# The first FFN block's plain product, its two weights and the left sums moved ahead, around the last dense unit

## Chip, cores and metric

One core of a Trainium2 (trn2) chip. The metric is device time of one execution in microseconds (us), the median of several runs; lower is better. Times inside an execution are us from its first instruction.

## The reference, cut to what matters

Two layers, 256 tokens, model width 2048, FFN width 5632, all float32. Each layer is a mixer followed by a SwiGLU FFN, with RMS norms around both.

```python
def swiglu(h, w_gate, w_up, w_down):
    return (jax.nn.silu(h @ w_gate) * (h @ w_up)) @ w_down

for layer in range(DEPTH):
    h = rms_norm(x, norm_mix_pre[layer])
    m = ...                                  # even_mixer or diff_attention_mixer
    x = x + rms_norm(m, norm_mix_post[layer])
    h = rms_norm(x, norm_ffn_pre[layer])
    f = swiglu(h, ffn_w_gate[layer], ffn_w_up[layer], ffn_w_down[layer])
    x = x + rms_norm(f, norm_ffn_post[layer])
```

## The kernel before

**Units.** All weights go by in tiles of 512x512 floats (1 MB). Every tile that TensorE (PE) uses is a numbered unit `u`, and each unit passes the same chain: SyncE's queue (SP) loads it into a raw buffer (`load`, line 770); ScalarE (ACT) rounds it into `w_hi` (`hi`, line 901); VectorE (DVE) puts the remainder into `w_lo` (`lo`, line 1495); PE multiplies `w_hi` with the high part of the activations, `w_lo` with the high part, and `w_hi` with the low part, in this order. A dense unit (`product`, line 1225) does this for both halves of the tokens (24 matmuls), a single product (`single`, line 1246) for one (12 matmuls). PE, ACT, DVE, POOL (GpSimd) and SP each run their own list of instructions strictly in order, and wait for one another by counters. `hi(u)` waits for the unit four before to be done, `lo(u)` for the unit three before.

**The FFN of a layer.** The 5632 columns are 11 blocks of 512. The first block is the head: eight dense units, `head[0..3]` for gate and `head[4..7]` for up (512 rows each). The other ten are bodies (`Body`, line 105) of fifteen entries each, `ENTRIES` (line 98): row blocks 0 and 1 of gate and up, for the first and the second 128 tokens, make a 2x2 by 2x2 block product that is computed with seven single products instead of eight, P1 to P7; row blocks 2 and 3 go through the dense units g2, g3, u2, u3; then d0 to d3 add the previous block's down product.

- The plain products P1, P2, P3 use the weight tiles g0, g1, u1 as loaded. P5, P6, P7, P4 use differences that DVE forms in place (`form`, line 1502): P5 from u0 - g0 in g0's buffer, P6 and P4 from that buffer again, P7 in u0's buffer. So g0's buffer is in use from P1 until the remainder of P4 has been taken.
- P5, P6, P7, P3 need sums of activations, S1 to S4 (the left sums). For the first body POOL computes all of them in one task (`left_sums`, line 1971: eight operations of 128x512, in the order S1, S3, S2, S4), ACT takes the high parts (`left_high`, line 1115), DVE the low parts (`left_low`, line 1525). POOL starts as soon as the norm's scale is there, whatever the place in the task list; the place counts for ACT and DVE.

**The order around the change.** It is written out by a planner. `head_end` (line 294) lists the tasks of `head[4..7]`, which every engine then filters for its own. For DVE the list is: remainder of `head[6]`; of `head[7]`; then in the slot of `head[6]` remainder of P1, form P5, remainder of P5; in the slot of `head[7]` left lows S1 and S3, then `gate_up` (line 1767, the product of silu(gate) and up into `tok`), left lows S2 and S4. After it comes the first body's own list (`block`, lines 1780 to 1857): form P6, remainders of P3, P6, g2, form P7, an addition, remainder of P2, form P4, remainders of P7, P4, u3, and so on. PE's order is `head[7]`, P1, P5, eight transposes of `tok` (`turn`, line 1426), P3, P6, g2, P2, P7, P4, u3, g3, u2, d0 to d3.

**Loads.** SP issues the loads in one order: the head's as its slots come, then `gains` (a broadcast vector into `gq`), then `LOADS` (line 99) of each body: u1, u0, g0, g2, g1, u3, g3, u2, d0, d1, d3, d2. `place_loads` (line 505) gives each load the buffer whose last load was taken longest ago: three raw buffers for the dense units, five in the bodies (the three, and `gx` and `queries`, which the attention uses before). A load waits until the buffer's former tile is no longer needed; for g0 that is the remainder of P4, for u1 the remainder of P3 and form P7, for u0 the remainder of P7, for a plain tile its own remainder. In the first body u1 and u0 go to `gx` and `queries`, g0, g2, g1 to the raw buffers, and u3 follows u1 in `gx`, g3 follows u0, u2 follows g0.

Of the kernel before, what the change touches and what calls it, by code (L numbers as in the profile page):

```python
# [31 lines left out]
P = 128  # L32
# [3 lines left out]
KC = 512  # L36
# [60 lines left out]

ENTRIES = ("P1", "P5", "P3", "P6", "g2", "P2", "P7", "P4", "u3", "g3", "u2", "d0", "d1", "d2", "d3")
LOADS = ("u1", "u0", "g0", "g2", "g1", "u3", "g3", "u2", "d0", "d1", "d3", "d2")
FORMS = ("P5", "P6", "P7", "P4")  # L100
SUMS = ("S2", "S3")
PLAIN = {"P1": "g0", "P2": "g1", "P3": "u1"}
# [2 lines left out]
class Body:  # L105


    def __init__(self, layer, j, index, u, n, e, m, n_head):

        self.layer, self.j, self.index, self.first = layer, j, index, j == 0  # L110
        self.base, self.e, self.m = u, e, m
        self.u = {name: u + i for i, name in enumerate(ENTRIES)}
        self.up, self.gate, self.down = n, n + 1, n + 2
        self.head_up, self.next = n_head + 1, None
        self.form = {name: len(FORMS) * index + i + 1 for i, name in enumerate(FORMS)}
        self.sum = {name: len(SUMS) * index + i + 1 for i, name in enumerate(SUMS)}


class Part:
# [174 lines left out]
def head_end(slots, body):  # L294

    def left(name):
        return Task("sums", 2 * body.layer + 1, body.layer, what=name)

    tasks = []
    for i, s in enumerate(slots):  # L300
        last = len(slots) - 1 - i
        tasks += half(s, 0)
        tasks += [hi(u) for u in range(ahead(s.u - 1, HI_LEAD), min(ahead(s.u, HI_LEAD), body.base + 1))]
        tasks += [lo(u) for u in range(ahead(s.u - 1, LO_LEAD), min(ahead(s.u, LO_LEAD), body.base + 1))]
        if last == 1:
            tasks += [Task("form", src=body, what="P5"), hi(body.base + 1), lo(body.base + 1)]
        if last == 0:
            tasks += [left("S1"), left("S3")]
        tasks += half(s, 1) + s.post
    return tasks + [left("S2"), left("S4")]  # L310


def boundary_tasks(b):
# [138 lines left out]
def make_plan():  # L452
    plan, before = Plan(), None
    for layer in range(2):
        slots = mixer_slots(plan, layer)
        plan.heads_of.append(plan.heads)
        n_gate, n_up = plan.n, plan.n + 1
        head = [plan.slot(w, kg, n, kg == 0, kg == NC - 1, layer=layer)
                for w, n in (("gate", n_gate), ("up", n_up)) for kg in range(NC)]
        for b, part in ((2 * layer, slots), (2 * layer + 1, head)):  # L460
            for slot in part:
                slot.b = b
        head[NC - 1].post.append(Task("silu", 2 * layer + 1, n=n_gate, u=head[NC - 1].u))
        head[-1].post += [Task("gate_up", n=n_gate, u=head[-1].u), Task("gains", 2 * layer + 2)]
        bodies = [Body(layer, j, plan.bodies + j, plan.u + len(ENTRIES) * j, plan.n + 2 + 6 * j, 0, 0, n_gate)
                  for j in range(NF - 1)]
        for body, after in zip(bodies, bodies[1:]):
            body.next = after
        plan.bodies += NF - 1
        plan.u += len(ENTRIES) * (NF - 1)  # L470
        plan.n += 6 * NF
        n_start = NC if before else 2 * NC
        start = boundary(2 * layer, before, slots[:NC]) if before else first_boundary(slots[:n_start])
        tasks = (start + run(slots[n_start:-NC]) + boundary(2 * layer + 1, slots[-NC:], head[:NC]) + head_end(head[NC:], bodies[0]))
        number(plan, tasks)
        plan.parts.append(Part(layer, tasks=tasks))
        for j in range(NF - 1):
            body = bodies[j]
            body.e, body.m = plan.e, plan.m
            plan.e += NT  # L480
            plan.m += NT
        plan.parts.append(Part(layer, bodies=bodies, tail=Tail(plan.e, plan.m)))
        assert plan.e % 2 == 0 and plan.n % 2 == 0
        plan.e += NT
        plan.m += NT
        for t in range(NT):
            plan.read["tok", t] = plan.e - NT + t
        before = [plan.slot("down", 0, plan.n - NC + cb, True, True, cb=cb, region="y", layer=layer) for cb in range(NC)]
        for slot in before:
            slot.block_e, slot.block_m = plan.e - NT, plan.m - NT  # L490
    tasks = last_boundary(4, before)
    number(plan, tasks)
    plan.parts.append(Part(tasks=tasks))
    place_loads(plan)
    return plan

# [8 lines left out]
def place_loads(plan):  # L505

    count, free, age = [0] * BLOCK_RAW, [()] * BLOCK_RAW, list(range(BLOCK_RAW))
    order = 0

    def take(key, buffers, released):  # L510
        nonlocal order
        buf = min(buffers, key=lambda i: age[i])
        count[buf] += 1
        plan.place[key] = Place(buf, count[buf], free[buf])
        free[buf] = released
        order += 1
        age[buf] = BLOCK_RAW + order

    age[3:] = [-2, -1]
    for part in plan.parts:  # L520
        for task in part.tasks or ():
            if task.kind == "tile_unit" or task.kind == "half" and task.t == 0 and task.passes[0] == 0:
                take(task.slot.u, range(RAW), (("lo", task.slot.u + 1),))
        for body in part.bodies or ():
            lo_of = {name: ("lo", u + 1) for name, u in body.u.items()}
            form_of = {name: ("form", n) for name, n in body.form.items()}
            released = {"g0": (lo_of["P4"],), "u0": (lo_of["P7"],), "u1": (lo_of["P3"], form_of["P7"]),
                        "g1": (lo_of["P2"], form_of["P4"])}
            for name in LOADS:
                take((body.index, name), range(BLOCK_RAW), released.get(name) or (lo_of[name],))  # L530
            for name in FORMS:
                plan.formed[body.u[name]] = body.form[name]
            for name in ENTRIES:
                weight = {"P4": "g0", "P5": "g0", "P6": "g0", "P7": "u0"}.get(name) or PLAIN.get(name, name)
                plan.place[body.u[name]] = plan.place[body.index, weight]


def trunk(nc, x, norm_mix_pre, norm_mix_post, norm_ffn_pre, norm_ffn_post,
# [9 lines left out]
    with ExitStack() as ctx:  # L548
# [215 lines left out]
        def _(sp):  # L764
# [44 lines left out]
            def gains(b):  # L809
# [6 lines left out]
                post = norm_mix_post[b // 2] if b % 2 else norm_ffn_post[b // 2 - 1]  # L816
                sp.dma_start(post_gain, post.partition_broadcast(P)).then_inc(gain_in, 16)

            def load_slot(slot):
                block = NF - 1 if slot.w == "down" else slot.kg  # L820
                rows = slice(block * KC, (block + 1) * KC)
# [6 lines left out]
            def task_of(task):  # L828
                if task.kind == "tile_unit" or task.kind == "half" and task.t == 0 and task.passes[0] == 0:
                    load_slot(task.slot)  # L830
                elif task.kind == "gains":
                    gains(task.b)
                elif task.kind == "input":
# [20 lines left out]
            for part in plan.parts:  # L854
                if part.tasks:
                    for task in part.tasks:
                        task_of(task)
                    continue
                wg, wu, wd = (weights[w][part.layer] for w in ("gate", "up", "down"))

                def block_load(body, name):

                    cols, rows = slice((body.j + 1) * KC, (body.j + 2) * KC), slice(body.j * KC, (body.j + 1) * KC)
                    k = int(name[1])
                    if name[0] == "d":
                        src = wd[rows, k * KC:(k + 1) * KC]
                    else:
                        src = (wg if name[0] == "g" else wu)[k * KC:(k + 1) * KC, cols]
                    load((body.index, name), src)

                sp.wait_ge(s_done, plan.heads_of[part.layer])
                for body in part.bodies:
                    for name in LOADS:
                        block_load(body, name)
            sp.wait_ge(stored, 16 * 5)

# [321 lines left out]
        def _(pe):  # L1198
# [47 lines left out]
            def single(u, bank, a_hi, a_lo, start, stop):  # L1246
# [9 lines left out]
                            mm.then_inc(half_done, 1)  # L1256
                mm.then_inc(unit_done, 1)

            def transposes(e, pieces):

                if e >= 2:
# [8 lines left out]
            def task_of(task):  # L1270
# [13 lines left out]
                elif task.kind == "T":  # L1284
# [18 lines left out]
                        transposes(task.e, [(input_tile(task.e, k), src[:, task.t, k * P:(k + 1) * P]) for k in range(KT)])  # L1303
                    else:
                        transposes(task.e, quarter(task.e, src, task.t))
                elif task.kind == "tile_unit":
                    tile_unit(task.slot)
                elif task.kind == "par" and task.i == 0:
# [69 lines left out]
            for part in plan.parts:  # L1378
# [7 lines left out]
                    pe.wait_ge(*ready)  # L1386
                    transposes(e + t, quarter(e + t, tok, t))

                def rows(kg, t):
                    return [b[:, kg * KT:(kg + 1) * KT, t * P:(t + 1) * P] for b in (h_hi, h_lo)]  # L1390

                def open_bank(body, name, column, t):

                    if name == first_of(column, t):
# [14 lines left out]
                def formed(body, name, bank, rows_of, start, stop):  # L1409
# [5 lines left out]
                        rows_of = (left_hi[left], left_lo[left])  # L1415
                    single(body.u[name], bank, *rows_of, start, stop)

                def down(body, j):

                    for t in range(NT):  # L1420
# [3 lines left out]
                def block(body):  # L1424
# [10 lines left out]
                    for name in ENTRIES:  # L1435
                        if name == "P1":
                            if not body.first:
                                pe.wait_ge(copied[0], body.index)
                            formed(body, name, product1, rows(0, 0), True, True)
                        elif name == "P5":  # L1440
                            if not body.first:
                                pe.wait_ge(copied[1], body.index)
# [609 lines left out]
```

## Time and profile before

| | |
|---|---|
| median of 3 runs | 2233.23 us (2232.08 to 2234.36) |
| the profiled execution's own time | 2234.35 us |
| its span, first to last instruction | 2232.6 us |
| busy: PE, DVE, ACT, POOL | 99%, 76%, 53%, 14% of the span |
| mean granted TensorE clock | 0.997 |
| DMA | 416.52 MB, mean 187 GB/s |
| the FFN head of layer 0 ends, its first body begins | 427.24 us |
| the same in layer 1 | 1557.37 us |

The profiled execution took 1.75 us more than its span and 1.1 us more than the median of the runs. In the timeline views a row stands for one or more like instructions (their start, the time from the first's start to the last's end, engine, line, output<-inputs, count), with the engine's idle time ahead of them and what ended it in brackets. Four matmuls of a pass overlap: such a row says about 1.07, while the next pass starts 0.91 later. "DVE w_lo L1499" is a remainder (`lo`), "ACT w_hi L909" a rounding (`hi`), "L1512" to "L1519" are the forms, "L1528" and "L1118" the left sums' low and high parts, "L1773" is `gate_up`.

### The profile page before, as it was taken

How to read it: one execution, taken by the hardware profiler on the slowest of the kernel's cores; microseconds unless marked ns; L12 is line 12 of the kernel's file. 1: busy time of each engine (PE TensorE's matmuls, PEld its weight loads, DVE VectorE, ACT ScalarE, POOL GpSimd, SP SyncE). 2: the span in 40 equal slices, each digit the busy share in tenths (PEclk: the TensorE clock that was granted, in tenths of full speed). 3: DMA queues.
4: the chain of work that ended last, by engine and by line, in shares of the span. 5: the costliest groups of instructions: out<-in, count | busy, mean ns of one | idle time of the engine just before them, and what ended most of it. 6: DMA issues, size and time to landing. Idle time of an engine off the chain costs nothing.

```text
span 2232.6 us, 26301 instructions
## 1 busy us (share of the span) xinstructions
PE 2202.4 (99%) x10011; PEld 1812.0 (81%) x10011; DVE 1688.6 (76%) x1680; ACT 1176.9 (53%) x1330; POOL 309.9 (14%) x253
## 2 busy tenths in 40 slices
PE   8999999999999999999999999999999999999998
PEld 6888888788888888888787888787788888888886
DVE  5587467788888888888746555777888888888886
ACT  6677545545554444454655555546454444444543
POOL 0851001200000000000121001003000000000001
PEclk9999999999999999999999999999999999999999
DMA  8545444466564445664564545455565445565543
GB/s 306 184 162 172 167 132 151 170 226 226 189 225 174 172 171 205 222 226 152 177 214 137 170 151 169 170 169 191 196 219 186 173 171 204 208 226 204 211 170 113
DMA packets 213883, 416.52 MB, mean 187 GB/s; under 512 B 12328, under 2 KB 14976, under 8 KB 213248
## 3 DMA queue, kind: packets, MB, share of 16 engines
q1 hardware_dynamic: 213040, 414.29, 53.0%
q8 instruction: 81, 1.33, 0.2%
q10 hardware_dynamic: 720, 0.56, 0.1%
q14 instruction: 42, 0.34, 0.0%
HBM read 412.73 MB, written 2.10 MB: 186 GB/s over the span
## 4 chain that ended last, share of the span: by engine, by line
PE 92%; DVE 3%; DMA 2%; issue 1%; ACT 1%; SPq 1%; ACTq 0%; POOLq 0%; POOL 0%; DVEq 0%
PE acc L1241 69%; PE acc L1254 12%; PE tp L1264 2%; PE sc L1254 2%; PE pv L1254 2%; DMA raw<-in_ffn_w_gate 1%; PE sc L1344 1%; DVE w_lo L1499 1%; PE pv L1373 1%; PE sc L1340 1%; DMA raw<-in_ev_w_in 1%; PE pv L1368 1%; ACT w_hi L909 0%; DMA yacc<-in_x_T 0%; PE sc L1323 0%
## 5 line engine op out<-in xcount | busy, mean ns | idle before, releaser
L909 ACT ACTIVATE w_hi<-raw 128x2048 fp32r<-128x2048 f32 x321 | 612.9, 1915 | 454.8 <-DVE raw L1512 93.4
L1499 DVE TENSOR_TENSOR w_lo<-raw,w_hi 128x2048 fp32r<-128x2048 f32 x321 | 735.8, 2303 | 134.8 <-ACT w_hi L909 92.3
L1241 PE MATMUL acc<-w_hi,h_hi 128*128 128x512 f32 x1576 | 431.5, 396 | 4.4 <-ACT h_hi L955 2.7
L1241 PE MATMUL acc<-w_hi,h_lo 128*128 128x512 f32 x1576 | 423.3, 390 | 1.6 <-DVE h_lo L1537 1.4
L1241 PE MATMUL acc<-w_lo,h_hi 128*128 128x512 f32 x1576 | 422.6, 390 | 1.1 <-DVE w_lo L1499 1.1
L1241 PEld LDWEIGHTS acc<-w_hi,h_lo 128*128 128x128 f32 x1576 | 295.9, 188 | 64.9 <-DVE h_lo L1537 2.7
L1241 PEld LDWEIGHTS acc<-w_lo,h_hi 128*128 128x128 f32 x1576 | 296.0, 188 | 64.1 <-DVE w_lo L1499 1.6
L1241 PEld LDWEIGHTS acc<-w_hi,h_hi 128*128 128x128 f32 x1576 | 291.1, 188 | 64.6 <-issue 6.7
L1241 PE MATMUL acc<-w_hi,y_hi 128*128 128x512 f32 x832 | 224.5, 392 | 0.7 <-ACT y_hi L1113 0.7
L1241 PE MATMUL acc<-w_lo,y_hi 128*128 128x512 f32 x832 | 222.6, 389 | 0.0
L1241 PE MATMUL acc<-w_hi,y_lo 128*128 128x512 f32 x832 | 222.5, 389 | 0.0
L2002 POOL TENSOR_TENSOR probT<-probT,rgx 128x512 f32<-128x512 f32 x20 | 40.8, 2040 | 1143.0 <-ACT rgx L1148 1143.0
L1579 DVE TENSOR_TENSOR yacc<-acc,yacc 128x512 f32<-128x512 f32 x208 | 138.7, 686 | 76.0 <-PE acc L1241 76.0
L1241 PEld LDWEIGHTS acc<-w_lo,y_hi 128*128 128x128 f32 x832 | 156.2, 188 | 32.7
L1241 PEld LDWEIGHTS acc<-w_hi,y_lo 128*128 128x128 f32 x832 | 156.2, 188 | 32.5
L1241 PEld LDWEIGHTS acc<-w_hi,y_hi 128*128 128x128 f32 x832 | 155.1, 188 | 32.9 <-issue 1.6
L909 ACT ACTIVATE w_hi<-queries 128x2048 fp32r<-128x2048 f32 x60 | 115.0, 1916 | 122.3 <-DVE queries L1512 34.6
L909 ACT ACTIVATE w_hi<-gx 128x2048 fp32r<-128x2048 f32 x60 | 114.9, 1916 | 121.4 <-DVE gx L1512 34.7
L1499 DVE TENSOR_TENSOR w_lo<-gx,w_hi 128x2048 fp32r<-128x2048 f32 x60 | 137.2, 2286 | 17.1 <-ACT w_hi L909 17.1
L1499 DVE TENSOR_TENSOR w_lo<-queries,w_hi 128x2048 fp32r<-128x2048 f32 x60 | 137.2, 2286 | 16.1 <-ACT w_hi L909 16.1
L1254 PE MATMUL acc<-w_hi,lefts 128*128 128x512 f32 x320 | 88.6, 399 | 0.0
L1016 ACT ACTIVATE probT<-tp 128x256 f32<-128x256 f32 (+1 forms) x48 | 22.0, 457 | 114.6 <-PE pv L1373 65.0
(250 smaller groups left out, 2315.6 us busy)
## 6 DMA issues: line engine op xcount, KB each, us to landing
raw<-in_ffn_w_gate SPq DMA_DIRECT2D x56, 1024.0 KB, 5.3
raw<-in_ffn_w_up SPq DMA_DIRECT2D x56, 1024.0 KB, 6.7
raw<-in_ffn_w_down SPq DMA_DIRECT2D x56, 1024.0 KB, 10.3
raw<-in_od_w_in SPq DMA_DIRECT2D x48, 1024.0 KB, 5.1
raw<-in_ev_w_in SPq DMA_DIRECT2D x37, 1024.0 KB, 5.2
raw<-in_ev_w_out SPq DMA_DIRECT2D x16, 1024.0 KB, 5.1
gx<-in_ffn_w_up SPq DMA_DIRECT2D x16, 1024.0 KB, 7.0
queries<-in_ffn_w_up SPq DMA_DIRECT2D x16, 1024.0 KB, 7.2
```

The costliest lines, as they stand in the source:

```text
L909: act.activation(w_hi[u % HI][:, :, :], raw[place.buf][:, :, :], ACT.Copy).then_inc(hi_done, 1)
L1016: act.activation(flat_pt[:, 0:cols], flat_tp[:, 0:cols], ACT.Copy).then_inc(tp_free[task.e % 2], 1)
L1241: mm = pe.matmul(acc[n % 2][t][:, :], operand(lhs, a, k, t), w[:, k, :], start=first and k == 0 and j == 0, stop=last and k == KT - 1 and ...
L1254: mm = pe.matmul(bank, a[:, k, :], w[:, k, :], start=start and k == 0 and j == 0, stop=stop and k == KT - 1 and j == 2)
L1264: ins = pe.transpose(dst, src, ident[:, :])
L1340: mm = pe.matmul(sc[:, t, :], q[:, kt, t * P:(t + 1) * P], k[:, kt, task.i % 2, :], start=True, stop=True)
L1344: mm = pe.matmul(sc[:, :, :].rearrange("p m t -> p (m t)"), q[:, kt, t * P:(t + 1) * P], k[:, kt, :, :].rearrange("p m t -> p (m t)"), sta ...
L1368: mm = pe.matmul(pv[:, 0, t * HD:(t + 1) * HD], probT[:, j, t * P:(t + 1) * P], v[:, j, task.i * HD:(task.i + 1) * HD], start=j == 0, stop ...
L1373: mm = pe.matmul(pv[:, 0, 0:CV], flat_pt[:, j * P:(j + 1) * P], v[:, j, hd * CV:(hd + 1) * CV], start=j == 0, stop=j == 1)
L1499: dve.tensor_tensor(w_lo[u % LO][:, :, :], raw[plan.place[u].buf][:, :, :], w_hi[u % HI][:, :, :].bitcast(F32), ALU.subtract).then_inc(lo_ ...
L1579: dve.tensor_tensor(y, a, y, ALU.add).then_inc(acc_free[n % 2][t], 1)
L2002: pool.tensor_tensor(spare[1], spare[1], spare[3], ALU.add).then_inc(spread, 1)
```

## The change

1. In the first body of each layer P1 changes places with `head[7]`: P1 becomes the unit before the last dense one, on every engine, and PE multiplies it ahead of `head[7]` (`first_product`).
2. The loads of g0 and u0 of the first body are issued by SP ahead of `head[4]`'s load, with the wait for the attention's last use of `gx` and `queries` ahead of them, and go to these two buffers (`early_load`). Their age in the buffer choice is raised by `EARLY_LEAD`. The other ten loads follow in the old order, u1, g2, g1, u3, g3, u2, d0, d1, d3, d2.
3. The left sums' parts, all four in the order S1, S3, S2, S4, stand in the slot of `head[6]`, behind the remainder of `head[7]`; form P5 with its rounding and remainder stands behind them in the slot of `head[7]`, and `gate_up` behind that.

```diff
+EARLY = ("g0", "u0")
+EARLY_LEAD = 5.5
@@ class Body
+        if self.first:
+            self.u["P1"] = u - 1
+def loads_of(body):
+    return tuple(name for name in LOADS if not (body.first and name in EARLY))
@@ def head_end(slots, body)
-    tasks = []
+    def ahead_of(slot, before, lead):
+        return range(ahead(before, lead), min(ahead(slot.u, lead), body.u["P5"]))
+
+    tasks, before = [], slots[0].u - 1
     for i, s in enumerate(slots):
-        last = len(slots) - 1 - i
+        if i == 0:
+            tasks += [Task("early_load", src=body, what=name) for name in EARLY]
+        if i == len(slots) - 1:
+            tasks.append(Task("first_product", src=body))
         tasks += half(s, 0)
-        tasks += [hi(u) for u in range(ahead(s.u - 1, HI_LEAD), min(ahead(s.u, HI_LEAD), body.base + 1))]
-        tasks += [lo(u) for u in range(ahead(s.u - 1, LO_LEAD), min(ahead(s.u, LO_LEAD), body.base + 1))]
-        if last == 1:
-            tasks += [Task("form", src=body, what="P5"), hi(body.base + 1), lo(body.base + 1)]
-        if last == 0:
-            tasks += [left("S1"), left("S3")]
+        tasks += [hi(u) for u in ahead_of(s, before, HI_LEAD)] + [lo(u) for u in ahead_of(s, before, LO_LEAD)]
+        before = s.u
+        if i == len(slots) - 2:
+            tasks += [left("S1"), left("S3"), left("S2"), left("S4")]
+        if i == len(slots) - 1:
+            tasks += [Task("form", src=body, what="P5"), hi(body.u["P5"]), lo(body.u["P5"])]
         tasks += half(s, 1) + s.post
-    return tasks + [left("S2"), left("S4")]
+    return tasks
@@ make_plan
+        head[-1].u += 1
@@ def place_loads(plan)
-    def take(key, buffers, released):
+    def take(key, buffers, released, later=0):
...
-        age[buf] = BLOCK_RAW + order
+        age[buf] = BLOCK_RAW + order + later
...
+            if task.kind == "early_load":
+                take((task.src.index, task.what), range(RAW, BLOCK_RAW), released(task.src, task.what), EARLY_LEAD)
...
-            for name in LOADS:
+            for name in loads_of(body):
@@ SyncE
+                elif task.kind == "early_load":
+                    if task.what == EARLY[0]:
+                        sp.wait_ge(s_done, plan.heads_of[task.src.layer])
+                    block_load(task.src, task.what)
...
-                sp.wait_ge(s_done, plan.heads_of[part.layer])
                 for body in part.bodies:
-                    for name in LOADS:
+                    for name in loads_of(body):
                         block_load(body, name)
@@ TensorE
+            def first_product(body):
+                single(body.u["P1"], product1, *rows(0, 0), True, True)
...
+                elif task.kind == "first_product":
+                    first_product(task.src)
...
                         if name == "P1":
                             if not body.first:
                                 pe.wait_ge(copied[0], body.index)
-                            formed(body, name, product1, rows(0, 0), True, True)
+                                first_product(body)
```

## Rows read from the trace of the kernel before

**Rows 1.** Page, part 1: busy us, share of the span, instructions

```profile
PE 2202.4 (99%) x10011; PEld 1812.0 (81%) x10011; DVE 1688.6 (76%) x1680; ACT 1176.9 (53%) x1330; POOL 309.9 (14%) x253
```

**Rows 2.** Waits of PE, whole run: us in total, times, longest

```profile
PE acc L1254 <- DVE w_lo L1499: 5.4, 2, 2.7
PE pv L1254 <- DVE y_lo L1528: 3.7, 2, 2.6
```

**Rows 3.** Timeline of PE, layer 0: end of head[5]; P1, P5, P3, P6, u3

```profile
415.45 1.07 PE L1241 MATMUL acc<-w_hi,h_lo 128*128 128x512 f32 x4
...
427.24 1.07 PE L1254 MATMUL sc<-w_hi,h_hi 128*128 128x512 f32 x4
...
432.68 1.19 PE L1254 MATMUL pv<-w_hi,y_hi 128*128 128x512 f32 x4 [2.56 <-DVE y_lo L1528]
...
440.21 1.20 PE L1254 MATMUL acc<-w_lo,lefts 128*128 128x512 f32 x4 [2.70 <-DVE w_lo L1499]
...
442.19 1.08 PE L1254 MATMUL acc<-w_hi,y_hi 128*128 128x512 f32 x4
...
459.63 1.07 PE L1241 MATMUL acc<-w_lo,h_hi 128*128 128x512 f32 x4
```

**Rows 4.** The same in layer 1

```profile
1557.37 1.07 PE L1254 MATMUL sc<-w_hi,h_hi 128*128 128x512 f32 x4
...
1568.94 2.08 PE L1254 MATMUL acc<-w_lo,lefts 128*128 128x512 f32 x4 [2.71 <-DVE w_lo L1499]
...
1572.23 1.09 PE L1254 MATMUL acc<-w_hi,y_hi 128*128 128x512 f32 x4
...
1589.58 1.07 PE L1241 MATMUL acc<-w_lo,h_hi 128*128 128x512 f32 x4
```

**Rows 5.** Busy time by stretch, layer 1; the third number from the end is PEclk

```profile
1568.90:1569.90 1.00, 0.96 (x2) 0.83 (x3) 1.00 (x1) 1.00 (x1) 0.00 (x0) 0.50 0.00 0
```

**Rows 6.** Timeline of ACT, layer 0: rounding of P1; high part of S4

```profile
421.31 1.92 ACT L909 ACTIVATE w_hi<-raw 128x2048 fp32r<-128x2048 f32 x1 [10.00 <-DMA raw<-in_ffn_w_gate]
...
431.16 0.62 ACT L1118 ACTIVATE lefts<-probT 128x512 fp32r<-128x512 f32 x1
```

**Rows 7.** Timeline of DVE, layer 0, from the remainder of head[5] to that of P4

```profile
404.68 4.50 DVE L1499 TENSOR_TENSOR w_lo<-raw,w_hi 128x2048 fp32r<-128x2048 f32 x2
...
411.34 2.39 DVE L1499 TENSOR_TENSOR w_lo<-raw,w_hi 128x2048 fp32r<-128x2048 f32 x1 [2.17 <-ACT w_hi L909]
...
423.26 2.29 DVE L1499 TENSOR_TENSOR w_lo<-raw,w_hi 128x2048 fp32r<-128x2048 f32 x1 [9.52 <-ACT w_hi L909]
...
433.15 1.40 DVE L1773 SCALAR_TENSOR_TENSOR tok<-acc,small,stage 128x512 f32<-128x512 f32 x2
...
435.07 0.68 DVE L1528 TENSOR_TENSOR lefts<-probT,lefts 128x512 fp32r<-128x512 f32 x1
435.67 2.28 DVE L1514 TENSOR_TENSOR raw<-gx,raw 128x2048 f32<-128x2048 f32 x1
...
453.88 2.28 DVE L1499 TENSOR_TENSOR w_lo<-raw,w_hi 128x2048 fp32r<-128x2048 f32 x1
```

**Rows 8.** Timeline of POOL, layer 0: the left sums, four of their eight operations

```profile
407.50 2.83 POOL L1980 TENSOR_TENSOR probT<-h_hi,h_lo 128x512 f32<-128x512 f32 x1
...
411.66 3.22 POOL L1987 TENSOR_TENSOR prob<-prob,probT 128x512 f32<-128x512 f32 x1
...
416.21 1.28 POOL L1990 TENSOR_TENSOR rgx<-rgx,probT 128x512 f32<-128x512 f32 x1
...
420.19 1.29 POOL L1996 TENSOR_TENSOR probT<-probT,rgx 128x512 f32<-128x512 f32 x1
```

**Rows 9.** Timeline of SP, layer 0: loads of head[2], head[3]; then of head[4..7]

```profile
366.88 6.34 SPq L775 DMA_DIRECT2D raw<-in_ffn_w_gate  x2
380.71 23.88 SPq L775 DMA_DIRECT2D raw<-in_ffn_w_up  x4
```

**Rows 10.** DMA issues from 446 to 447 us (u3): count, KB, us to landing

```profile
gx<-in_ffn_w_up SPq DMA_DIRECT2D x1, 1024.0 KB, 4.9
```

More of the change, by code:

```diff
@@ L516, in take, with released @@
         order += 1
-        age[buf] = BLOCK_RAW + order
+        age[buf] = BLOCK_RAW + order + later
+    def released(body, name):
+        lo_of = {entry: ("lo", u + 1) for entry, u in body.u.items()}
+        form_of = {entry: ("form", n) for entry, n in body.form.items()}
+        return {"g0": (lo_of["P4"],), "u0": (lo_of["P7"],), "u1": (lo_of["P3"], form_of["P7"]),
+                "g1": (lo_of["P2"], form_of["P4"])}.get(name) or (lo_of[name],)
     age[3:] = [-2, -1]
@@ L521, in place_loads @@
         for task in part.tasks or ():
-            if task.kind == "tile_unit" or task.kind == "half" and task.t == 0 and task.passes[0] == 0:
+            if task.kind == "early_load":
+                take((task.src.index, task.what), range(RAW, BLOCK_RAW), released(task.src, task.what), EARLY_LEAD)
+            elif task.kind == "tile_unit" or task.kind == "half" and task.t == 0 and task.passes[0] == 0:
                 take(task.slot.u, range(RAW), (("lo", task.slot.u + 1),))
         for body in part.bodies or ():
[L525 to L528, printed above, removed]
-            for name in LOADS:
-                take((body.index, name), range(BLOCK_RAW), released.get(name) or (lo_of[name],))
+            for name in loads_of(body):
+                take((body.index, name), range(BLOCK_RAW), released(body, name))
             for name in FORMS:
@@ L817, in gains, with block_load @@
                 sp.dma_start(post_gain, post.partition_broadcast(P)).then_inc(gain_in, 16)
+            def block_load(body, name):
+                cols, rows = slice((body.j + 1) * KC, (body.j + 2) * KC), slice(body.j * KC, (body.j + 1) * KC)
+                k = int(name[1])
+                if name[0] == "d":
+                    src = weights["down"][body.layer][rows, k * KC:(k + 1) * KC]
+                else:
+                    src = weights["gate" if name[0] == "g" else "up"][body.layer][k * KC:(k + 1) * KC, cols]
+                load((body.index, name), src)
             def load_slot(slot):
@@ L858, in _ @@
                     continue
[L859 to L869, printed above, removed]
-                sp.wait_ge(s_done, plan.heads_of[part.layer])
                 for body in part.bodies:
-                    for name in LOADS:
+                    for name in loads_of(body):
                         block_load(body, name)
@@ L1257, in single, with rows @@
                 mm.then_inc(unit_done, 1)
+            def rows(kg, t):
+                return [b[:, kg * KT:(kg + 1) * KT, t * P:(t + 1) * P] for b in (h_hi, h_lo)]
+            def first_product(body):
+                single(body.u["P1"], product1, *rows(0, 0), True, True)
             def transposes(e, pieces):
@@ L1387, in down_operand @@
                     transposes(e + t, quarter(e + t, tok, t))
-                def rows(kg, t):
-                    return [b[:, kg * KT:(kg + 1) * KT, t * P:(t + 1) * P] for b in (h_hi, h_lo)]
                 def open_bank(body, name, column, t):
```

## The prediction

> **What bounds the kernel now.** I read the busy shares first: PE works in 99% of the span [rows 1], so only PE's idle time, or work of PE itself, can move the end. The change adds and drops no matmul. Next the list of who waited for whom: PE's whole idle time at the head of the bodies is two kinds of wait, once a layer each, 9.1 us together: P5 on the left sum S1, and P3 on its remainder [rows 2]. Then PE's timeline across that place. In layer 0 P1 starts at 427.24 and P6 at 442.19, 14.95 us later, with waits of 2.56 and 2.70; without them it would be 9.7 [rows 3]. In layer 1 the same way takes 14.86: the first wait is shorter, but the four matmuls after the second take 2.08 instead of 1.20, at a granted clock of 0.50, which is 1.2 GHz; from the resumption to P6 there are 3.29 us, in layer 0 1.98, so the clock cost 1.31 [rows 3 to 5]. So some 5.2 us a layer can be won here, 10.4 in all.
>
> Why PE waits is read on the other engines. P1's rounding waits for the load of g0, after 10.0 us in which ACT has nothing to do [rows 6]; behind it DVE takes P1's remainder at 423.26, after 9.5 idle us, forms P5, and only then the left sums' low parts, `gate_up` and, at 435.67, form P6, from where it is busy without a gap until the remainder of P4 ends at 456.16 [rows 7]. So g0's late load is the root, and from P5 to u3 DVE is the second bound: 20.49 us from form P6 to the end of P4's remainder.
>
> **The change, part by part (layer 0).**
>
> *The early loads.* SP issues head[3]'s load by 373.2 and stands still until head[4]'s at 380.71 [rows 9]; g0 and u0 go between. A load that is alone lands in 4.9 us [rows 10]. Even with all three one behind the other (14.7 us) head[4] lands by 395.4, and PE comes to it four units of 5.44 before P1, at 405.48 [rows 3]. The wait on the attention that is now ahead of head[4] has long been met there. Cost nothing; were that cover gone, head[4] would be late by what lands after some 401.
>
> *P1 ahead of head[7].* The same twelve matmuls, 2.72 us, in another place. P1's rounding and remainder take the place of head[7]'s, about 409.4 to 413.7 [rows 7]; head[7]'s remainder needs head[5] done, 416.52 [rows 3]. PE needs them at 421.8 and 425.4. Nothing.
>
> *The left sums.* They stood where POOL had long been done: its eight operations end at 421.48 [rows 8], the first low part came after 431. Now DVE's four low parts come straight behind head[7]'s remainder, and form P5 is queued behind the last of them: DVE stands until POOL has finished, which it did not before. And POOL will not keep its pace. Its operations take 1.28 alone, but 2.83 and 3.22 beside a remainder on DVE, and each ended 1.15 after that remainder did (409.18 to 410.33, 413.73 to 414.88) [rows 7, 8]: as good as no progress beside it. Before, DVE was idle from 413.7 to 423.26 and POOL ran free; now head[7]'s remainder falls into this stretch. POOL's operation of 416.21 is running, DVE begins when it ends, about 417.4, and is through at 419.6; POOL's next ends at 420.75, two more of 1.35 from start to start give 423.5. The three short low parts (S1, S3, S2, some 0.6 each) can hold it up once each: 425.3. No row shows a short one beside POOL. Bounds: 421.5 (no hold-up at all) and 425.3; I take 424.5, two of the three, since the hold-up by long ones is complete in both rows.
>
> The Trainium skill ("SBUF — State Buffer", "SBUF: two separate sides") has a rule for this: VectorE and GpSimd share one port pair, and the one that starts first holds it for its whole instruction, the other blocked; two inputs in SBUF are enough on VectorE's side. By that rule the low parts block as well, and the sum below would be 1.6 us larger over both layers. The two rows agree for the long operations.
>
> *From the sums to form P6.* S4's high part 0.62 and low part 0.68 put form P5 at 425.8; form 2.28, rounding 1.92, remainder 2.29, `gate_up` 1.40 [rows 6, 7] put form P6 at 433.7, only 2.0 earlier than before. PE meanwhile has finished head[7] at 429.96, waits 1.4 in P5, reaches P3 at 434.9, waits there for the remainder until 433.7 + 4.4 = 438.1 and starts P6 at 439.9. Here the change is ahead by 2.3 us.
>
> *What is late next: u3.* The buffer choice takes the oldest. Counting loads from g0 = 0: g0 5.5, u0 6.5 (raised), head[4..7] 2 to 5 in three buffers, the first reused by head[7]. u1, g2 and g1 then go to the buffers of head[5], head[6] and head[7] (3, 4, 5), and the next oldest is g0's, 5.5, against 6 for u1's. So u3 goes into g0's buffer, which is free only after P4's remainder. Before, u3 followed u1 and was issued at form P7's end. SP is in order: g3, u2, d0 and d1 wait behind it too. On DVE u3's remainder is the next entry after P4's, so the whole way of the load is open: DVE is continuous from form P6 as before, P4's remainder ends at 433.7 + 20.5 = 454.2, landing 4.9, rounding 1.92, remainder 2.29 and 0.1 for handing over give 463.4. PE is through P4 at 456.0, idle until the rounding is there, 461.0, and after the first pass again until 463.4. Before, this second pass of u3 began at 459.63 [rows 3]: 3.8 later. In layer 1 P1 starts 1130.13 later than in layer 0, and the POOL and DVE work that sets the sums is tied to it: 1593.5 against 1589.58 [rows 4], 3.9 later. The loads behind u3 land one after the other while PE works through u3, and DVE and ACT catch up in the bodies, but PE has no idle time there to give the loss back.
>
> *Clock.* The wait of 5.0 ahead of u3 is twice those of [rows 3], none of which brought the clock down there; in layer 1 a shorter one did, for 1.31 [rows 4]. Bounds 0 and 1.3 a layer; I take 0.7, a fall whose first pass hides in the wait for the remainder. The Trainium skill ("TensorE: Matmul & The Clock Gate", "Part 1: The HAM clock gate") says that idleness brings the half rate and activity lifts it; by it the fall is certain, the row agrees, and the sum would take 1.3 at both places.
>
> *Sum:* 3.8 + 3.9 + 2 x 0.7 = 9.1. The profiled execution would go from 2234.35 to 2243.5; the median, 1.1 lower, from 2233.2 to **2242.3**. With the bounds (sums at 423.5 to 425.3, clock 0 to 2.6) the forecast's own range is 2238.9 to 2245.1.
>
> **The rivals.**
>
> *POOL keeps its pace* (sums done at 421.5): everything on DVE is 3.0 earlier, u3's second pass at 460.4. Still late by 0.8 and 1.0: +1.8, 2235.0. For it: DVE's share of the port may be yielded between instructions. Against it: [rows 7, 8]. This is inside 0.2% (4.5 us, about what a measurement can tell from no change). That the change in effect does nothing, since DVE comes to P4's remainder about when it did, ends in the same place. 0.18 together.
>
> *u3 comes in time* (the other side). If u3 does not wait for g0's buffer but is issued at form P7's end, as before, the gain at P6 stays. Its price: 2.3 and 2.1 a layer with the sums at 424.5, 5.2 a layer if POOL also keeps its pace (form P6 at 430.7, P3's remainder at 435.1): 2228.8 to 2222.8, taken as 2226. It decides at the issue of u3: 459.63 less 4.9, 1.92, 2.29 is 450.5; whatever lets it go before that makes the change win. For it: the wins at P5 and P3 are real in [rows 3]. Against it: the ages above leave no other buffer. 0.10.
>
> *More than the sum:* POOL is held up by all three low parts, and the clock falls at P3 and u3 alike: up to +12, 2245.2, and some more if the burst of five loads slows u3's own. It is the upper end of the forecast's mechanism, 0.06 of its chance.
>
> **How the numbers follow.** Forecast 0.72 with its upper end, no gain and no loss 0.18, in time 0.10. The range takes in the forecast and the first rival, 2234.5 to 2246.5, and leaves out the winning case and a little above. Slower by over 0.2%: 0.72; within: 0.18; faster: 0.10.
>
> **What would show it.** Right: in PE's waits, P5's on the low part is gone; a wait of some 5 us ahead of u3 (L1241) on ACT's rounding stands in both layers, and one of 1.4 on its remainder; ACT's idle time ahead of that rounding is ended by the DMA of u3 into `gx`, issued within 0.1 us of the end of P4's remainder; POOL's last sum ends near 424.5; DVE waits ahead of the last low parts for ACT; a low clock just after u3's start. Wrong: u3's issue some 9 us ahead of P4's remainder, POOL's last sum still at 421.5, or P6 starting less than 2 or more than 4 us earlier than at 442.19.

## The result, and the profile after

The changed kernel takes 2243.23 us (median of 6 runs, 2242.06 to 2246.56) against 2233.36 for the kernel before (6 runs): 9.9 us more, ratio 1.0045, 95% interval [1.0032, 1.0058]. So it is slower by more than 0.2%. The profiled execution took 2242.28 us, its span is 2240.5. At the place of the change its layer 0 stands 2.33 us earlier than that of the kernel before, and has done so since before the change acts (POOL's sums begin at 405.17, in [rows 8] at 407.50; SP's load of head[2] at 364.55, in [rows 9] at 366.88). In layer 1 it stands 3.35 later (P1 begins at 1555.28, where before head[7] began, 5.44 ahead of the 1557.37 of [rows 4]), at the end 7.9 later. So layer 0 cost 5.7 us and layer 1 4.6.

The list of PE's waits after, us in total, times, longest:

```profile
PE acc L1262 <- ACT w_hi L930: 9.0, 2, 4.5
PE acc L1275 <- DVE w_lo L1526: 3.6, 2, 1.8
...
PE pv L1275 <- DVE w_lo L1526: 2.1, 2, 1.1
```

The wait of [rows 2] on a low part of the left sums is gone; P5 now waits 1.07 for its own remainder, and P3's wait has come down from 2.7 to 1.80. In exchange there is a wait that did not exist: 4.5 us a layer on ACT's rounding. The timeline of PE in layer 0 says which unit it is (start, us, engine, line, operation, count, idle time before and what ended it):

```profile
419.46 1.07 PE L1275 MATMUL sc<-w_hi,h_hi 128*128 128x512 f32 x4
...
435.50 1.21 PE L1275 MATMUL acc<-w_lo,lefts 128*128 128x512 f32 x4 [1.80 <-DVE w_lo L1526]
...
437.48 1.07 PE L1275 MATMUL acc<-w_hi,y_hi 128*128 128x512 f32 x4
...
453.13 1.07 PE L1275 MATMUL acc<-w_hi,h_lo 128*128 128x512 f32 x4
458.69 2.08 PE L1262 MATMUL acc<-w_hi,h_hi 128*128 128x512 f32 x4 [4.49 <-ACT w_hi L930]
461.02 2.08 PE L1262 MATMUL acc<-w_lo,h_hi 128*128 128x512 f32 x4 [0.25 <-DVE w_lo L1526]
...
467.42 1.07 PE L1262 MATMUL acc<-w_hi,h_hi 128*128 128x512 f32 x4
```

With 2.33 added, P6 starts at 439.81 instead of 442.19 [rows 3]: up to there the change has won 2.4 us. Then u3 comes, and its second pass is at 463.35 instead of 459.63 [rows 3]: 3.7 lost. In layer 1 the same pass starts at 1596.82, or 1593.47 without the 3.35, against 1589.58 [rows 4]: 3.9 lost.

```profile
1594.49 2.03 PE L1262 MATMUL acc<-w_hi,h_hi 128*128 128x512 f32 x4 [4.46 <-ACT w_hi L930]
1596.82 1.72 PE L1262 MATMUL acc<-w_lo,h_hi 128*128 128x512 f32 x4 [0.30 <-DVE w_lo L1526]
...
1602.04 1.07 PE L1262 MATMUL acc<-w_hi,h_hi 128*128 128x512 f32 x4
```

What u3 waits for stands in the timelines of DVE (P4's remainder, then u3's), SP and ACT, again in layer 0:

```profile
449.18 2.29 DVE L1526 TENSOR_TENSOR w_lo<-gx,w_hi 128x2048 fp32r<-128x2048 f32 x1
458.67 2.29 DVE L1526 TENSOR_TENSOR w_lo<-gx,w_hi 128x2048 fp32r<-128x2048 f32 x1 [7.21 <-ACT w_hi L930]
```

```profile
451.49 0.37 SPq L795 DMA_DIRECT2D gx<-in_ffn_w_up  x1
451.96 0.45 SPq L795 DMA_DIRECT2D raw<-in_ffn_w_gate  x1
452.45 0.51 SPq L795 DMA_DIRECT2D queries<-in_ffn_w_up  x1
```

```profile
456.73 1.91 ACT L930 ACTIVATE w_hi<-gx 128x2048 fp32r<-128x2048 f32 x1 [7.72 <-DMA gx<-in_ffn_w_up]
```

P4's remainder ends at 451.47 (449.18 + 2.29). SP issues u3 into `gx`, where g0 lay, 0.02 us later, and g3 and u2 right behind it. The load lands 5.2 us after its issue, the rounding takes 1.91, and DVE, which has stood idle for 7.21 us, begins u3's remainder. The timeline of POOL shows the sums (the last four of eight operations), that of DVE what ran against them (head[7]'s remainder, the four low parts, form P5, form P6):

```profile
413.88 1.29 POOL L2017 TENSOR_TENSOR rgx<-rgx,probT 128x512 f32<-128x512 f32 x1
415.24 3.22 POOL L2019 TENSOR_TENSOR rgx<-prob,rgx 128x512 f32<-128x512 f32 x1
418.42 1.74 POOL L2007 TENSOR_TENSOR probT<-h_hi,h_lo 128x512 f32<-128x512 f32 x1
420.24 1.62 POOL L2023 TENSOR_TENSOR probT<-probT,rgx 128x512 f32<-128x512 f32 x1
```

```profile
414.29 3.02 DVE L1526 TENSOR_TENSOR w_lo<-raw,w_hi 128x2048 fp32r<-128x2048 f32 x1 [2.89 <-PE acc L1262]
417.23 1.78 DVE L1555 TENSOR_TENSOR y_lo<-prob,y_hi 128x512 fp32r<-128x512 f32 x1
418.94 1.77 DVE L1555 TENSOR_TENSOR lefts<-rgx,lefts 128x512 fp32r<-128x512 f32 x1
420.63 1.78 DVE L1555 TENSOR_TENSOR y_lo<-rgx,y_hi 128x512 fp32r<-128x512 f32 x1
422.56 0.69 DVE L1555 TENSOR_TENSOR lefts<-probT,lefts 128x512 fp32r<-128x512 f32 x1 [0.15 <-ACT lefts L1139]
423.17 2.28 DVE L1539 TENSOR_TENSOR gx<-queries,gx 128x2048 f32<-128x2048 f32 x1
...
430.97 2.28 DVE L1541 TENSOR_TENSOR gx<-raw,gx 128x2048 f32<-128x2048 f32 x1
```

POOL's last sum ends at 421.86, that is 424.19 on the old axis, where it ended at 421.48 [rows 8]. Form P6 starts at 430.97, or 433.30, instead of 435.67 [rows 7]. Last, the granted clock behind the wait for u3, in stretches of layer 0 and of layer 1 (length, then busy us of PE, its weight load, DVE, ACT, POOL; then the clock, the share of DMA, GB/s):

```profile
461.00:462.00 1.00, 0.98 (x2) 0.83 (x3) 1.00 (x2) 0.35 (x1) 0.00 (x0) 0.50 1.06 393
...
465.00:466.00 1.00, 1.00 (x6) 0.83 (x5) 1.00 (x1) 0.54 (x1) 0.00 (x0) 1.00 1.05 387
```

```profile
1596.80:1597.80 1.00, 0.98 (x2) 0.83 (x3) 1.00 (x2) 0.35 (x1) 0.00 (x0) 0.50 1.03 383
...
1598.80:1599.80 1.00, 1.00 (x6) 0.79 (x6) 0.76 (x1) 1.00 (x1) 0.00 (x0) 1.00 1.06 389
```

### The profile page after: what moved, and what is told of

Its sections match the earlier page's. It is cut to its first block, busy times and chain, and to the rows that moved or that the text cites. A ratio compares the mean times of both kernels' runs of the same rounds, so it can differ in the third digit from the quotient of the medians.

```text
span 2240.5 us, 26301 instructions
## 1 busy us (share of the span) xinstructions
PE 2206.4 (98%) x10011; PEld 1815.1 (81%) x10011; DVE 1695.9 (76%) x1680; ACT 1177.5 (53%) x1330; POOL 314.1 (14%) x253
## 4 chain that ended last, share of the span: by engine, by line
PE 93%; DVE 3%; DMA 1%; issue 1%; SPq 1%; ACT 1%; POOLq 0%; POOL 0%; DVEq 0%; ACTq 0%
PE acc L1262 71%; PE acc L1275 11%; PE sc L1275 2%; PE tp L1291 2%; PE pv L1275 2%; DVE w_lo L1526 2%; PE sc L1373 1%; DMA raw<-in_ev_w_in 1%; PE pv L1402 1%; PE sc L1369 1%; PE pv L1397 1%; DMA gx<-in_ffn_w_up 0%; ACT w_hi L930 0%; PE sc L1352 0%; PE pv L1352 0%
## 5 line engine op out<-in xcount | busy, mean ns | idle before, releaser
L930 ACT ACTIVATE w_hi<-gx 128x2048 fp32r<-128x2048 f32 x66 | 126.6, 1918 | 158.8 <-DVE gx L1539 40.9
L1526 DVE TENSOR_TENSOR w_lo<-gx,w_hi 128x2048 fp32r<-128x2048 f32 x66 | 151.5, 2295 | 38.7 <-ACT w_hi L930 34.7
L930 ACT ACTIVATE w_hi<-queries 128x2048 fp32r<-128x2048 f32 x54 | 103.4, 1915 | 84.5 <-DMA queries<-in_ffn_w_gate 18.2
L1526 DVE TENSOR_TENSOR w_lo<-queries,w_hi 128x2048 fp32r<-128x2048 f32 x54 | 123.5, 2286 | 13.7 <-ACT w_hi L930 13.7
## 6 DMA issues: line engine op xcount, KB each, us to landing
raw<-in_ffn_w_down SPq DMA_DIRECT2D x56, 1024.0 KB, 10.4
```

Source lines behind the costliest of these rows:

```text
L930: act.activation(w_hi[u % HI][:, :, :], raw[place.buf][:, :, :], ACT.Copy).then_inc(hi_done, 1)
L1526: dve.tensor_tensor(w_lo[u % LO][:, :, :], raw[plan.place[u].buf][:, :, :], w_hi[u % HI][:, :, :].bitcast(F32), ALU.subtract).then_inc(lo_ ...
```

## The experiments

The theory after the result: u3 behind P4's remainder turns a gain of 2.4 us a layer into a loss; POOL's hold-up takes another part of the gain; the early loads are the source of the gain, and the swap of P1 is not needed. The rivals: the order of the sums, or the swap, makes the loss. Each time is a median, each ratio is to the kernel before on the same chip.

| run | us | ratio [95% interval] |
|---|---|---|
| buffer_alone | 2246.96 | 1.0065 [1.0052, 1.0077] |
| changed_again | 2244.00 | 1.0051 [1.0037, 1.0064] |
| sums_behind_form | 2240.57 | 1.0039 [1.0026, 1.0052] |
| busy_wait | 2239.39 | 1.0035 [1.0022, 1.0047] |
| loads_alone | 2239.14 | 1.0027 [1.0016, 1.0037] |
| u3_own_buffer | 2228.38 | 0.9983 [0.9974, 0.9991] |
| both_undone | 2226.19 | 0.9974 [0.9963, 0.9984] |
| loads_alone_own_buffer | 2223.68 | 0.9962 [0.9947, 0.9976] |

The kernel before stood at 2232.02 in the set of four (u3_own_buffer, sums_behind_form, both_undone, busy_wait), at 2232.97 beside the two loads_alone kernels and at 2232.54 beside the other two.

**u3_own_buffer.** The changed kernel, only the ages differ:

```diff
-EARLY_LEAD = 5.5
+EARLY_LEAD = {"g0": 6.7, "u0": 5.5}
...
-                take(..., released(task.src, task.what), EARLY_LEAD)
+                take(..., released(task.src, task.what), EARLY_LEAD[task.what])
```

> The changed kernel with one difference: g0 and u0 get ages (6.7 and 5.5) by which u3 follows u1, g3 follows u0 and u2 follows g0, as in the kernel before. Theory (u3 waits for g0's buffer, and this alone turns the gain into a loss): the wait of some 4.5 us ahead of u3 is gone in both layers, POOL's sums and P6 stay where they are in the changed kernel, and PE is ahead of the kernel before by 2.4 us a layer from P6 on: 4.7 us faster than before, about 2228.6. Rival (the load is late for another reason, SP's order or the queue): u3's wait stays, about 2243.

Measured: 2228.38, ratio 0.9983, 3.6 us faster than before, where 4.7 was expected. PE's timeline of layer 0 (P4's last pass, then u3's three passes for the first tokens):

```profile
452.15 1.07 PE L1275 MATMUL acc<-w_hi,h_lo 128*128 128x512 f32 x4
453.05 1.07 PE L1262 MATMUL acc<-w_hi,h_hi 128*128 128x512 f32 x4
453.96 1.07 PE L1262 MATMUL acc<-w_lo,h_hi 128*128 128x512 f32 x4
454.87 1.07 PE L1262 MATMUL acc<-w_hi,h_lo 128*128 128x512 f32 x4
```

No wait between P4 and u3. SP's timeline has the reason, u3's load now goes to a raw buffer and leaves 9.4 us before the one that takes g0's:

```profile
441.15 0.37 SPq L795 DMA_DIRECT2D raw<-in_ffn_w_up  x1
...
450.51 0.37 SPq L795 DMA_DIRECT2D gx<-in_ffn_w_up  x1
```

The buffer that u3 takes, with g3's and u2's that change along with it, is the difference between slower and faster than before.

**buffer_alone.** The kernel before, only the ages of u1 and u0 differ:

```diff
-                take((body.index, name), range(BLOCK_RAW), released.get(name) or (lo_of[name],))
+                take((body.index, name), range(BLOCK_RAW), released.get(name) or (lo_of[name],),
+                     {"u1": 2.2, "u0": 1.5}.get(name, 0) if body.first else 0)
```

(`take` adds the fourth value to the age, as in the change.)

> The kernel before with nothing but the buffer choice changed: u1 and u0 of the first body get ages raised by 2.2 and 1.5, so that u3 takes g0's buffer, g3 takes u1's and u2 u0's, as in the changed kernel; no early load, no swap, sums where they were. Theory (u3 behind the remainder of P4 exposes its whole way): PE waits some 4.7 us ahead of u3 in both layers, u3's second pass 6.0 us later in layer 0 and 4.8 in layer 1 than before, with 0.7 to 1.9 a layer for the clock some 13 us slower than the kernel before, about 2246. Rival (DVE and ACT have slack enough at u3, and the loss of the change came from the order of the sums): no change, 2233.

Measured: 2246.96, ratio 1.0065. PE's waits of this run:

```profile
PE acc L1242 <- ACT w_hi L910: 7.8, 2, 4.6
PE pv L1255 <- DVE y_lo L1529: 4.0, 2, 2.6
PE acc L1255 <- DVE w_lo L1500: 3.8, 2, 2.7
```

The waits at P5 and P3 are still there (P3's in layer 0 is 1.10 instead of 2.70, since P5 ahead of it fell to the low clock, its second pass 1.65 instead of 1.08), and the one ahead of u3 stands beside them (4.64 in layer 0, 3.20 in layer 1, where 4.7 was expected for both). Counted from P1's start, u3's second pass comes 6.3 and 5.3 us later than before, for 6.0 and 4.8. With none of the change's other parts the buffer choice costs 14 us: the cause is shown in both directions.

**sums_behind_form.** The changed kernel with the old order of form P5 and the left sums' parts:

```diff
         if i == len(slots) - 2:
-            tasks += [left("S1"), left("S3"), left("S2"), left("S4")]
+            tasks += [Task("form", src=body, what="P5"), hi(body.u["P5"]), lo(body.u["P5"])]
         if i == len(slots) - 1:
-            tasks += [Task("form", src=body, what="P5"), hi(body.u["P5"]), lo(body.u["P5"])]
+            tasks += [left("S1"), left("S3")]
         tasks += half(s, 1) + s.post
-    return tasks
+    return tasks + [left("S2"), left("S4")]
```

> The changed kernel with the left sums' parts back behind form P5 and its remainder (S1, S3 ahead of gate_up, S2, S4 behind it), u3 still in g0's buffer. Theory (DVE's wait for POOL delays form P6 by a little over 1 us a layer, while u3's place costs the rest): form P6 some 1.3 us earlier a layer, u3's wait stays at 4.5 to 5 us, about 2240.6. Rival (the hold-up of POOL and of the left sums' low parts is the main cost): back to 2233 or less.

Measured: 2240.57. Form P6 starts 10.23 us after P1 (428.55 and 418.32) instead of 11.51: 1.28 a layer, as expected. PE waits 2.92 us ahead of u3 in layer 0, where 4.5 to 5 was expected (P3's second pass ran at the low clock, 1.76, and brought PE there later), and 4.65 in layer 1. Counted from P1's start, u3's second pass comes 1.4 and 1.1 us earlier than in the changed kernel, but the low clock behind it lasts longer, and at g3 only 0.5 and 0.1 are left. So the order of the sums is a term of the loss, but a small one, and the times alone do not show it: the intervals overlap, and that the median met the expected 2240.6 is partly luck, since 1.1 of the 1.7 us between the two profiled executions (spans 2238.8 and 2240.5) arose ahead of P1 (418.32 and 419.46). What the order costs is that DVE stands behind POOL's sums. POOL itself was slower here, not faster: its last sum ends 3.68 us after P1's start instead of 2.40, since form P5 then stood in its way (the same POOL operation as above at 418.42):

```profile
417.27 3.35 POOL L2007 TENSOR_TENSOR probT<-h_hi,h_lo 128x512 f32<-128x512 f32 x1
```

**both_undone.** The two edits together.

> Both together: old buffers for u3, g3, u2 and the left sums' parts behind form P5; P1 ahead of head[7] and the two early loads stay. Theory: the parts add up, form P6 at about 432.0 on the time axis of the kernel before, P6 3.9 us earlier a layer, no wait at u3: 7.7 us faster than before, about 2225.6. Rival (DVE, not the load, paces PE from P7 to u3, so that an earlier form P6 is given back): no better than the first run of this set, about 2228.6.

Measured: 2226.19, ratio 0.9974, 5.8 us faster than before, where 7.7 was expected. On DVE the parts add up: form P6 comes 10.23 us after P1's start in both layers (11.50 in u3_own_buffer), and nothing waits at u3. PE has the gain in one layer only. The wait for P3's remainder is followed by the low clock in layer 0 and not in layer 1 (PE's timeline, P3's second pass and P6's first):

```profile
434.50 1.87 PE L1275 MATMUL acc<-w_lo,lefts 128*128 128x512 f32 x4 [1.92 <-DVE w_lo L1526]
...
437.87 1.24 PE L1275 MATMUL acc<-w_hi,y_hi 128*128 128x512 f32 x4
```

```profile
1562.48 1.20 PE L1275 MATMUL acc<-w_lo,lefts 128*128 128x512 f32 x4 [1.92 <-DVE w_lo L1526]
...
1564.46 1.08 PE L1275 MATMUL acc<-w_hi,y_hi 128*128 128x512 f32 x4
```

So P6 comes 18.15 us after P1's start (419.72) in layer 0 and 16.75 (1547.71) in layer 1, against 18.02 in both layers of u3_own_buffer. The intervals of the two runs overlap, but this median lies below the lowest time of u3_own_buffer (2226.65).

**loads_alone** and **loads_alone_own_buffer.** Only the early loads: from sums_behind_form and both_undone the swap of P1 is taken out as well, and on PE P1 stands in the body's list again.

```diff
-        if self.first:
-            self.u["P1"] = u - 1
...
-        if i == len(slots) - 1:
-            tasks.append(Task("first_product", src=body))
...
-        head[-1].u += 1
```

> The kernel before with only the early loads of g0 and u0 (ages raised by 5.5 as in the change, so that u3 waits for g0's buffer); P1 behind head[7], the left sums' parts where they were. Theory (the late g0 is the root of PE's waits at P5 and P3, and the raised age costs at u3): form P6 at about 431 instead of 435.7, P5's wait gone and P3's down to about 1 us, then a wait of nearly 5 us ahead of u3 and its second pass 1.3 us later than before, plus the low clock: some 5 us slower than before, about 2238. Rival (the swap of P1 causes the loss): no slower than before, 2233 or less.

> The same with the ages 6.7 and 5.5, so that u3, g3, u2 follow u1, u0, g0 as before. Theory (the early loads are the whole gain, and the swap of P1 adds nothing): no wait at u3, P6 4.9 us earlier a layer, 9.7 us faster than before, about 2223.7, and so faster than the version that keeps the swap. Rival (P1 ahead of head[7] is needed for the gain): slower than that version, 2226 or more.

(The version that keeps the swap is both_undone.) Measured: 2239.14 and 2223.68, ratios 1.0027 and 0.9962. PE's waits of the second:

```profile
PE acc L1270 <- DVE w_lo L1521: 2.3, 2, 1.2
```

Between the head and u3 this, at P3, is the only wait left in either layer; loads_alone has it too, and 4.45 and 4.55 ahead of u3. P1 was at no time what held PE up; with its weight there in time, it is better placed behind head[7]. `gate_up` on DVE needs head[7]'s result, and with P1 ahead of head[7] its second half stands for it (DVE's timeline of both_undone, then form P6):

```profile
428.08 0.75 DVE L1800 SCALAR_TENSOR_TENSOR tok<-acc,small,stage 128x512 f32<-128x512 f32 x1 [0.68 <-PE acc L1262]
...
429.95 2.29 DVE L1541 TENSOR_TENSOR gx<-raw,gx 128x2048 f32<-128x2048 f32 x1
```

With P1 behind head[7] it does not wait (loads_alone_own_buffer):

```profile
425.37 1.39 DVE L1795 SCALAR_TENSOR_TENSOR tok<-acc,small,stage 128x512 f32<-128x512 f32 x2
...
427.89 2.27 DVE L1536 TENSOR_TENSOR gx<-raw,gx 128x2048 f32<-128x2048 f32 x1
```

Form P6 comes 9.47 us after the end of head[6] (418.42), in both_undone 10.23 (419.72), and P6 on PE 15.98 in both layers, for 18.15 and 16.75. The intervals of the two runs overlap ([0.9947, 0.9976] and [0.9963, 0.9984]); the order is shown by these rows. Of the change's three parts only the loads win.

**busy_wait.** The changed kernel with 36 matmuls more in each layer, into a bank that has been copied already, so that PE works through most of the wait for u3:

```diff
+                            if body.first:
+                                pe.wait_ge(copied[0], body.index + 1)
+                                for k in range(36):
+                                    pe.matmul(sc[:, 0, :], h_hi[:, k % 16, 0:P], h_hi[:, k % 16, :], start=True, stop=True)
```

> The changed kernel with 36 idle-time matmuls of 256 columns (4 us) into the first product's bank, already copied, between P4 and u3 of the first body: PE is kept at work in the wait for u3, nothing else changes. Theory (after this wait PE runs at 1.2 GHz, which costs 1.86 us in layer 0 and 0.68 in layer 1 of the changed kernel's trace): granted clock 1.00 at u3, passes of u3 at 1.07 instead of 2.08, about 2.5 us faster than the changed kernel, 2240.7. Rival (the slow passes hide in the waits for u3's remainder and the loads behind it): 2243.

Measured: 2239.39, ratio 1.0035. PE's timeline of layer 0:

```profile
453.35 4.47 PE L1486 MATMUL sc<-h_hi 128*128 128x256 f32 x36
458.02 1.20 PE L1262 MATMUL acc<-w_hi,h_hi 128*128 128x512 f32 x4 [0.20 <-ACT w_hi L930]
460.35 1.20 PE L1262 MATMUL acc<-w_lo,h_hi 128*128 128x512 f32 x4 [1.13 <-DVE w_lo L1530]
461.38 1.08 PE L1262 MATMUL acc<-w_hi,h_lo 128*128 128x512 f32 x4
...
465.02 1.07 PE L1262 MATMUL acc<-w_hi,h_hi 128*128 128x512 f32 x4
```

From u3's second pass to g3 it is 4.67 us in both layers, in the changed kernel 6.40 (461.02 to 467.42) and 5.22. The clock's part of the loss is shown by the passes; the times themselves (1.0035 here, 1.0051 and 1.0045 for the changed kernel) lie the right way with overlapping intervals.

**changed_again.** The changed kernel once more, beside buffer_alone.

> The changed kernel as it is, a second time, beside the run above and on the same chip. Every theory: 2242 to 2245; the wait ahead of u3 of 4.5 us and the low clock behind it stand in the trace again.

Measured: 2244.00; the wait ahead of u3 4.46 and 4.53, the first two passes behind it 2.08 and 2.08 in layer 0, 1.88 and 1.79 in layer 1.

## Why the prediction was right

*The early loads cost nothing:* right. SP issues g0 and u0 at 370.93 and 371.48 and head[4] at 378.37, on the old axis 380.70 as in [rows 9].

*P1 ahead of head[7] costs nothing on PE:* right, PE has no wait there. The 0.8 us a layer that the swap costs in both_undone is no part of the changed kernel's loss: there `gate_up` follows P5's remainder at 429.65 without a wait.

*POOL held up:* right in size, 424.19 for 424.5. The way there was somewhat different: not only does a short low part hold up POOL, POOL holds up the low part just as well. The three take 1.77 or 1.78 instead of 0.68, and the two engines go turn by turn. Head[7]'s remainder held POOL up by 1.9, two of the low parts by 0.45 and 0.33 (3.22, 1.74 and 1.62 instead of 1.29); the third came when POOL's last operation was already next. By its own figures "two of the three" made 424.7, not 424.5. The Trainium skill ("SBUF — State Buffer", "SBUF: two separate sides") has whichever starts first hold the shared port for its whole instruction, and the other blocked. These rows agree, for short operations too. But the 1.6 us that the prediction drew from this rule does not follow from it: with the low parts blocking in turn, the sums ended at 424.19, not 425.3.

*Form P6 and P6:* 433.30 for 433.7, 439.81 for 439.9. P3's wait was 1.80 for 2.3, P5's 1.07 for 1.4.

*u3:* right in both layers, 3.7 and 3.9 for 3.8 and 3.9. The load took 5.2 us for the 4.9 of [rows 10]; form P6 came 0.4 earlier: the two misses cancel, which is luck. The wait ahead of u3 was 4.5 for 5.0, because PE's end of P4 was put at 456.0; from P6 at 439.9 the 16.5 us of [rows 3] (442.19 to 459.63 less one pass of 0.91) lead to 456.4.

*The clock:* right that it falls, the term was mis-sized in layer 0. From u3's second pass to g3 it cost 1.86 there and 0.68 in layer 1 (6.40 and 5.22 against 4.54, five passes of 0.907), for 0.7 each. The bound of 1.3, from the one place of [rows 4], was too low. The wait of 1.4 for u3's remainder shows as 0.25 only because the first pass takes 2.08.

*The sum:* 3.7 + 1.9 + 3.9 + 0.7 = 10.2 by the trace and 9.9 by the medians, for 9.1. Of the rivals, "POOL keeps its pace" is out by POOL's rows, and "u3 comes in time" did not happen, but u3_own_buffer is this rival made true: its price was put at -4.4 to -10.4 and came to -3.6 in the medians, with P6 2.4 us ahead as in the changed kernel.

## What to carry to other kernels

A load that is moved ahead keeps its buffer longer, and somebody else's buffer choice changes with it: list which load follows which in every buffer, and see whether the tile that must be released last is still followed by a load that can wait. A round of hand-made ages can do this wrong by half a step, and the whole latency of a load, its rounding and its remainder then stand open. When a stall goes back to a late load, try the early load alone before reordering the work around it: here, with the old buffer choice, it was the whole gain (0.9962), and the reordering took part of it back.

## What the runs showed of the hardware that was not expected

Short VectorE and GpSimd operations on SBUF took turns: 128x512 ones of 0.68 and 1.29 us took 1.78 and 1.62 to 1.74 when they met, while a GpSimd one behind a 2.2 us remainder or form took 2.83 to 3.35 and ended 1.15 or 1.16 after it. And the low clock follows no simple order of waits: behind 4.45 us and more u3's first pass fell to 1.2 GHz in all eight places (1.88 to 2.08 instead of 1.20), yet in both_undone a wait of 1.92 ahead of P3 was followed by such passes in layer 0 (1.87) and not in layer 1 (1.20), and in [rows 3] neither 2.56 nor 2.70 was. Ahead of u3, 2.92 and 3.20 (sums_behind_form in layer 0, buffer_alone in layer 1) left the first pass at 1.20, and the second, after 1.13 more of waiting, took 2.08 and 2.07. The same wait cost 1.86 in one layer of the changed kernel and 0.68 in the other.
